# A chunkwise delta-rule recurrence on TensorE: the output products of one chunk are issued between the state products of the next

## The chip, the cores and the metric

The kernel runs on one core of one Trainium2 chip. The metric is device time in microseconds (us) of one execution, and the figure for a kernel is the median of its runs. Before the change that is 1708.27 us (three runs, 1707.21 to 1708.54).

## The reference, cut to what matters

The program is a two-layer encoder trunk for 512 frames of width 1024. The change lies in the gated DeltaNet heads of layer 0: 4 heads of 128 features, 8 chunks of 64 frames, one chunk after the other:

```python
def step(state, inp):
    u_c, wk_c, qk_c, qg_c, kt_c, dec_c = inp
    w = u_c - jnp.einsum('bhtd,bhde->bhte', wk_c, state)
    o = jnp.einsum('bhtd,bhde->bhte', qg_c, state) + jnp.einsum('bhtj,bhje->bhte', qk_c, w)
    state = dec_c[..., None, None] * state + jnp.einsum('bhtd,bhte->bhde', kt_c, w)
    return state, o
```

A chunk's w needs the state that the chunk before left. Its output o is needed by no later chunk, only by the normalisation and the output projection behind the loop.

## The kernel before, in words

Each engine has its own hand-written list of instructions, and semaphores join them; no scheduler moves anything. The recurrence is `rec_pe` (TensorE), `rec_dve` (VectorE) and `rec_act` (ScalarE), each a loop over the 8 chunks c. Two chunks share a 128-row tile i = c // 2: an even chunk's rows lie on partitions 0 to 63, an odd chunk's on 64 to 127 (`r`); `ro` is the other half.

For each chunk TensorE issues, in this order:

- L1325, "wk with state": per head a 128-row product to 64 output partitions, into banks 0 and 1 (two heads each). Between them L1328, "q with state", the first term of o, into bank 2 or 3 by the chunk's parity, on the other 64 output partitions. Both are done in two groups of two heads; a group waits for the state of its two heads (semaphore s_new), and L1325 of its second head counts r_ws up.
- L1333, "k with w": per head a product over the chunk's 64 rows to 128 output partitions, into banks 4 and 5. A group of two heads waits for its w (r_w) and counts r_kw up.
- L1336, "QK with w", the second term of o, added into the bank of L1328: per head a product over the same 64 rows to 64 output partitions. The last counts r_om up.

VectorE forms w from r_ws (L1350, two instructions of two heads), then the new state from r_kw (L1354, four instructions of one head); after chunks 3, 5 and 7 it also sums squares of an earlier output tile (L1376). w lies in two slots by parity, so L1350 of chunk c waits until r_om tells that chunk c - 2 is through. ScalarE copies o out of its bank (L1363, counts r_o) and squares it (L1366) after an odd chunk. L1325 of chunk c waits for the copy of chunk c - 2.

Behind the loop TensorE goes on with the output projection: 48 matmuls of the S5 half (L329 to L331) into banks 0 to 3, after r_o has counted all 8 chunks and GpSimd has split the S5 half (L1416, L1417, semaphore cat_s5); then the transposes of the normalised DeltaNet outputs (L1424), the DeltaNet half, and the rest of the program.

A fp32 matmul of these lines is recorded as two passes, each a weight load and a matmul: 4 heads give 8 records. The form that the profile prints before the operand shapes, such as 64*128, is rows by columns of the array that the instruction uses; 64*64 and 64*128 are L1336 and L1333, 128*64 is L1325 and L1328.

Of the kernel before, what the change touches and what calls it, by code (L numbers as in the profile page):

```python
# [10 lines left out]
ACT = mybir.ActivationFunctionType  # L11
AX = mybir.AxisListType.X

P = 128
# [19 lines left out]
GH = 4  # L34
GD = 128
NCH = SEQ // CHUNK
# [39 lines left out]
def build_program(nc, A):  # L76
    ctx = ExitStack()
    with ctx:
# [14 lines left out]
        ps = ctx.enter_context(nc.psum_tensor("ps", [P, 8, 512], F32))  # L93
# [32 lines left out]
        def named(name):  # L126

            if name in GOES_ON:
                return GOES_ON[name]
            head, _, tail = name.partition("_")  # L130
            for what, tags in SERIES.items():
                if head in tags and in_series(what, tail, head) is not None:
                    return f"{what}_{tail}", sum(in_series(what, tail, t) or 0 for t in tags[:tags.index(head)])
            if head[-1].isdigit() and f"{head[:-1]}_{tail}" in PER_LAYER:
                base_name = f"{head[:-1]}_{tail}"
                goes_on, n = GOES_ON.get(base_name, (base_name, 0))
                return goes_on, n + int(head[-1]) * PER_LAYER[base_name]
            return name, 0

        def sem(name):  # L140
            name = named(name)[0]
            if name not in sems:
                sems[name] = ctx.enter_context(nc.semaphore(name))
            return sems[name]


        def reg(at, *shape):
            n = 1
            for s in shape:
                n *= s  # L150
            v = sb[:, at - SB0:at - SB0 + n]
            if len(shape) == 2:
                v = v.rearrange("p (a b) -> p a b", a=shape[0])
            if len(shape) == 3:
                v = v.rearrange("p (a b c) -> p a b c", a=shape[0], b=shape[1])
            if len(shape) == 4:
                v = v.rearrange("p (a b c d) -> p a b c d", a=shape[0], b=shape[1], c=shape[2])
            return v
# [39 lines left out]
        CHUNKS = (slice(0, CHUNK), slice(CHUNK, P))  # L198
# [201 lines left out]
        def norm_pe(pe, t, x, h):  # L400

            n = x.shape[1]
            for k in range(KT):
                for i in range(n):
                    if k == 0:
                        pe.wait_ge(sem(f"{t}_hv"), after(f"{t}_hv", i + 1))
                    ins = pe.transpose(norm_bank(n, k)[:, i * P:(i + 1) * P], h[:, i, k * P:(k + 1) * P], ident)
                ins.then_inc(sem(f"{t}_turned"), 1)
# [224 lines left out]
        def logits_pe(pe):  # L633
            pe.wait_ge(sem("wab_lo"), 1)
            for k in range(KT):
                for part in range(2):
                    ins = pe.matmul(ps[0:4 * GH, 7, :], w_ab_split[:, k, :, :].rearrange("p a b -> p (a b)"), hT0[part][:, k, :],
                                    start=(k == 0 and part == 0), stop=(k == KT - 1 and part == 1))
            ins.then_inc(sem("logit_mm"), 1)
# [336 lines left out]
        q_gT = gd(TT, GH, P)  # L976
        AQ_T = gd(TT, 2, GH, CHUNK)
        U_m, Y_m, T_m, A_l = gd(TT, GH, CHUNK), gd(TT, GH, CHUNK), gd(TT, GH, CHUNK), gd(TT, GH, CHUNK)
        A_T, QK_T = AQ_T[:, :, 0], AQ_T[:, :, 1]
# [3 lines left out]
        state = gd(GH, GD)  # L983
        w_c = gd(2, GH * GD)
# [20 lines left out]
        u_n, wk_T, o_t = reg(qkv0, TT, GH, GD), reg(qkv0 + 2048, TT, GH, P), reg(qkv0 + 4096, TT, GH, GD)  # L1005
        flat3 = lambda a: a.rearrange("p a b -> p (a b)")
# [304 lines left out]
                              ps[:, 4 * (i % 2) + 2:4 * (i % 2) + 4, 0:SOLVE_W].rearrange("p c (h t) -> p c h t", h=GH)).then_inc(sem("wk_c"), 1)  # L1311


        def rec_pe(pe):
            for c in range(NCH):
                i, r, ro = c // 2, CHUNKS[c % 2], CHUNKS[1 - c % 2]
                for g in range(2):
                    pe.wait_ge(sem("s_new"), 1 + GH * (c - 1) + 2 * g + 2 if c else 1)
                    if c == 0 and g == 0:
                        pe.wait_ge(sem("u_c"), 2 * TT)  # L1320
                        pe.wait_ge(sem("wk_c"), TT)
                    if c >= 2 and g == 0:
                        pe.wait_ge(sem("r_o"), c - 1)
                    for h in (2 * g, 2 * g + 1):
                        ins = pe.matmul(ps[r, g, h * P:(h + 1) * P], wk_T[:, i, h, r], state[:, h, :], start=True, stop=True)  # L1325
                        if h == 2 * g + 1:
                            ins.then_inc(sem("r_ws"), 1)
                        pe.matmul(ps[ro, 2 + c % 2, h * P:(h + 1) * P], q_gT[:, i, h, r], state[:, h, :], start=(h == 0), stop=False,  # L1328
                                  skip_group_check=True)
                for g in range(2):  # L1330
                    pe.wait_ge(sem("r_w"), 2 * c + g + 1)
                    for h in (2 * g, 2 * g + 1):
                        ins = pe.matmul(ps[:, 4 + g, h * P:(h + 1) * P], k_t[r, i, h, :], w_c[r, c % 2, h * P:(h + 1) * P], start=True, stop=True)  # L1333
                    ins.then_inc(sem("r_kw"), 1)
                for h in range(GH):
                    ins = pe.matmul(ps[ro, 2 + c % 2, h * P:(h + 1) * P], QK_T[r, i, h, :], w_c[r, c % 2, h * P:(h + 1) * P],  # L1336
                                    start=False, stop=True, skip_group_check=True)
                ins.then_inc(sem("r_om"), 1)

        def rec_dve(v):  # L1340
            for c in range(NCH):
# [17 lines left out]
        def rec_act(a):  # L1359
            for c in range(NCH):  # L1360
                i, r = c // 2, CHUNKS[1 - c % 2]
                a.wait_ge(sem("r_om"), c + 1)
                a.activation(flat3(o_t[r, i]), ps[r, 2 + c % 2, :], ACT.Copy).then_inc(sem("r_o"), 1)  # L1363
                if c % 2 == 1:
                    a.wait_ge(sem("r_o"), c + 1)
                    a.activation(o_sq[:, i], o_t[:, i], ACT.Square).then_inc(sem("go_sq"), 1)  # L1366
# [1013 lines left out]
        @block.tensor  # L2380
        def _(pe):
            pe.wait_ge(sem("con_in"), 16)
            norm_pe(pe, "n0", x0, h0)
            ab_groups_pe(pe, 0, 3)
            logits_pe(pe)
            ab_groups_pe(pe, 4, 4)
            logits_turn_pe(pe)
            ab_groups_pe(pe, 5, 9)
            gates_pe(pe)
            ab_groups_pe(pe, 10, 12)  # L2390
            s5_tables_pe(pe)
            ab_groups_pe(pe, 13, 13)
            s5_tm_pe(pe)
            ab_groups_pe(pe, 14, 14)
            s5_states_pe(pe)
            ab_groups_pe(pe, 15, 19)
            gdn_squares_pe(pe)
            s5_out_pe(pe)
            s5_back_pe(pe)
            gdn_turn_pe(pe, 0)  # L2400
            gdn_prod_pe(pe, 0)
            s5_glu_pe(pe)
            pe.wait_ge(sem("glu_s"), 4)
            for i in range(TT):
                gdn_row_pe(pe, i)
                gdn_back_pe(pe, i)
                if i + 1 < TT:
                    gdn_turn_pe(pe, i + 1)
                    gdn_prod_pe(pe, i + 1)
            solve_pe(pe)  # L2410
            uw_pe(pe)
            rec_pe(pe)


            def cat_ready(k):
                if k == 0:
                    pe.wait_ge(sem("r_o"), NCH)
                    pe.wait_ge(sem("cat_s5"), 1)
                if k >= 4:
                    pe.wait_ge(sem("cat_lo"), after("cat_lo", k - 3))  # L2420

            rows_pe(pe, "mo", "abo0", cat, TT, 0, ready=cat_ready, between=lambda: gout_pe(pe))
            def mem_turn():
                pe.wait_ge(sem("mo_x"), after("mo_x", 4))
                norm_pe(pe, "m", mem_x, mem_x)

            rows_pe(pe, "mo", "abo1", cat, TT, 4, between=mem_turn)
            for l in range(DEPTH):
                if l == 0:
                    kv_pe(pe)  # L2430

                xq_pe(pe, l)
                xa_pe(pe, l)

                split_outproj_pe(pe, f"xo{l}", xo[l], oT[l], ready=lambda k: pe.wait_ge(sem(f"xa{l}_ov"), after(f"xa{l}_ov", k + 1)), between=lambda: turn_rows_pe(pe, f"f{l}", 0, f"xo{l}_x"))
                ffn_up_pe(pe, l)
                ffn_down_pe(pe, l)
                if l == 0:
                    ca_proj_pe(pe)
                    ca_turn_pe(pe)  # L2440
                    ca_pe(pe)
                    pe.wait_ge(sem("c_ol"), CH // 2)
                    split_outproj_pe(pe, "co", cao, c_oT, between=lambda: turn_rows_pe(pe, "x1", 0, "co_x"))
# [280 lines left out]
```

## Time and profile before

| what | value |
|---|---|
| median of three runs | 1708.27 us |
| profiled execution, its own time | 1708.71 us |
| its span | 1706.9 us |
| TensorE busy | 1648.6 us, 97% of the span |
| stretch of the recurrence | 284.4 to 311.1 us of the span, 8 chunks |
| TensorE matmul records in that stretch | 256 |
| granted TensorE clock in that stretch | 1.00 of full speed |

The span runs from the first to the last instruction that the profile holds; 1.8 us of the execution lie around it. Times in the rows below are microseconds from the start of the span. A matmul record's end is modelled, so spacing is read from the starts of records; busy shares of TensorE tell little, since a record lasts about 0.27 us even where the next starts 0.11 us after it.

### The profile page before, as it was taken

How to read it: one execution, taken by the hardware profiler on the slowest of the kernel's cores; microseconds unless marked ns; L12 is line 12 of the kernel's file. 1: busy time of each engine (PE TensorE's matmuls, PEld its weight loads, DVE VectorE, ACT ScalarE, POOL GpSimd, SP SyncE). 2: the span in 40 equal slices, each digit the busy share in tenths (PEclk: the TensorE clock that was granted, in tenths of full speed). 3: DMA queues.
4: the chain of work that ended last, by engine and by line, in shares of the span. 5: the costliest groups of instructions: out<-in, count | busy, mean ns of one | idle time of the engine just before them, and what ended most of it. 6: DMA issues, size and time to landing. Idle time of an engine off the chain costs nothing.

```text
span 1706.9 us, 22635 instructions
## 1 busy us (share of the span) xinstructions
PE 1648.6 (97%) x9358; PEld 1343.3 (79%) x9358; DVE 768.2 (45%) x1006; ACT 623.9 (37%) x1010; POOL 253.4 (15%) x315
## 2 busy tenths in 40 slices
PE   5989989999999999999999999999999999999999
PEld 4778788788878788888888887567887788888887
DVE  4658435555444444443225435773453444444222
ACT  6533433344434322221114336564452522222110
POOL 3863034010000211110000003110000011111000
PEclk9999899999999999999999999999999999999999
DMA  6610212034212333332223332322212243333221
GB/s 203 135 50 1 75 52 71 31 123 149 74 49 75 99 98 98 96 97 88 92 95 99 99 123 99 96 78 99 80 45 74 60 113 98 93 93 94 91 98 74
DMA packets 146801, 151.85 MB, mean 89 GB/s; under 512 B 8864, under 2 KB 109344, under 8 KB 146592
## 3 DMA queue, kind: packets, MB, share of 16 engines
q1 hardware_dynamic: 146720, 150.69, 28.9%
q8 instruction: 60, 0.98, 0.2%
q14 instruction: 21, 0.17, 0.0%
HBM read 147.53 MB, written 3.15 MB: 88 GB/s over the span
## 4 chain that ended last, share of the span: by engine, by line
PE 88%; DVE 6%; ACT 4%; issue 2%; POOL 0%; DMA 0%; SPq 0%; DVEq 0%; ACTq 0%; POOLq 0%
PE ps L329 24%; PE ps L331 24%; PE ps L330 24%; PE ps L2070 1%; PE ps L1730 1%; PE ps L425 1%; PE ps L2100 1%; DVE sb L610 1%; PE ps L1707 1%; PE ps L964 1%; DVE w_lo_ab L301 1%; PE ps L2088 1%; ACT sb L1741 1%; ACT sb L2159 1%; PE ps L1242 1%
## 5 line engine op out<-in xcount | busy, mean ns | idle before, releaser
L329 PE MATMUL ps<-h_hi,w_hi 128*128 128x512 f32 x864 | 338.7, 392 | 4.4 <-DVE w_lo L1904 3.9
L330 PE MATMUL ps<-h_lo,w_hi 128*128 128x512 f32 x864 | 337.2, 390 | 0.0
L301 DVE TENSOR_TENSOR w_lo<-raw,w_hi 128x2048 fp32r<-128x2048 f32 x66 | 155.0, 2349 | 341.7 <-ACT w_hi L297 341.7
L297 ACT ACTIVATE w_hi<-raw 128x2048 fp32r<-128x2048 f32 x84 | 160.8, 1915 | 377.1 <-PE ps L331 376.4
L331 PE MATMUL ps<-h_hi,w_lo 128*128 128x512 f32 x704 | 274.4, 390 | 0.0
L329 PEld LDWEIGHTS ps<-h_hi,w_hi 128*128 128x128 f32 x864 | 162.9, 189 | 39.2 <-issue 4.7
L330 PEld LDWEIGHTS ps<-h_lo,w_hi 128*128 128x128 f32 x864 | 162.9, 189 | 33.5
L1904 DVE TENSOR_TENSOR w_lo<-raw,w_hi 128x2048 fp32r<-128x2048 f32 x44 | 138.1, 3139 | 53.5 <-ACT w_hi L1886 53.5
L331 PEld LDWEIGHTS ps<-h_hi,w_lo 128*128 128x128 f32 x704 | 132.5, 188 | 27.8
L1886 ACT ACTIVATE w_hi<-raw 128x2048 fp32r<-128x2048 f32 x44 | 84.3, 1916 | 161.2 <-PE ps L331 161.2
L1914 POOL CAST a_hi<-up 128x512 f32 x44 | 27.0, 613 | 777.2 <-DVE up L1902 777.2
L329 PE MATMUL ps<-w_hi,a_hi 128*128 128x512 f32 x352 | 137.3, 390 | 1.7 <-DVE up L1902 1.7
L330 PE MATMUL ps<-w_lo,a_hi 128*128 128x512 f32 x352 | 137.0, 389 | 0.0
L331 PE MATMUL ps<-w_hi,a_lo 128*128 128x512 f32 x352 | 137.0, 389 | 0.0
L329 PE MATMUL ps<-w_hi,h_hi 128*128 128x512 f32 x320 | 125.0, 391 | 0.0
L331 PE MATMUL ps<-w_hi,h_lo 128*128 128x512 f32 x320 | 124.5, 389 | 0.0
L330 PE MATMUL ps<-w_lo,h_hi 128*128 128x512 f32 x320 | 124.5, 389 | 0.0
L1902 DVE TENSOR_TENSOR up<-up,ps 128x512 f32<-128x512 f32 x44 | 30.3, 688 | 192.6 <-PE ps L331 188.9
L1882 ACT ACTIVATE up<-up 128x512 f32<-128x512 f32 x44 | 27.8, 632 | 153.2 <-DVE up L1898 153.2
L329 PEld LDWEIGHTS ps<-w_hi,a_hi 128*128 128x128 f32 x352 | 66.1, 188 | 16.1 <-DVE up L1902 2.5
L331 PEld LDWEIGHTS ps<-w_hi,a_lo 128*128 128x128 f32 x352 | 66.1, 188 | 13.9
L330 PEld LDWEIGHTS ps<-w_lo,a_hi 128*128 128x128 f32 x352 | 66.1, 188 | 13.6
(378 smaller groups left out, 2697.3 us busy)
## 6 DMA issues: line engine op xcount, KB each, us to landing
raw<-in_f_w_gate SPq DMA_DIRECT2D x44, 512.0 KB, 4.0
raw<-in_f_w_up SPq DMA_DIRECT2D x44, 512.0 KB, 5.2
raw<-in_f_w_down SPq DMA_DIRECT2D x44, 512.0 KB, 4.2
raw<-in_xa_w_kv SPq DMA_DIRECT2D x16, 1024.0 KB, 5.0
raw<-in_c_w_qkv SPq DMA_DIRECT2D x12, 1024.0 KB, 5.1
raw<-in_ab_w_in SPq DMA_DIRECT2D x10, 1024.0 KB, 6.0
raw<-in_xa_w_q SPq DMA_DIRECT2D x8, 1024.0 KB, 5.0
raw<-in_xa_w_out SPq DMA_DIRECT2D x8, 1024.0 KB, 5.0
```

The lines of the kernel that those rows point to most:

```text
L297: a.activation(w_hi[:, n % 2, :], raw[n % 2], ACT.Copy).then_inc(sem("w_hi"), 1)
L301: v.tensor_tensor(w_lo(n)[:, n % 2, :], raw[n % 2], w_hi[:, n % 2, :].bitcast(F32), ALU.subtract).then_inc(sem("w_lo"), 1)
L329: pe.matmul(out, a[0], b[0], start=start, stop=False)
L330: pe.matmul(out, a[0], b[1], start=False, stop=False)
L331: return pe.matmul(out, a[1], b[0], start=False, stop=stop)
L425: ins = pe.transpose(ps[:, k, i * P:(i + 1) * P], x[:, i, k * P:(k + 1) * P], ident)
L610: ins = v.scalar_tensor_tensor(y[:, s:SEQ], b[:, 0:SEQ - s], pcol("conv", (3 - s) * 12 + n), y[:, s:SEQ], ALU.mult, ALU.add)
L1882: a.activation(gsil[:, s, :], gsil[:, s, :], ACT.Silu).then_inc(sem(f"f{l}_silu"), 1)
L1886: a.activation(w_hi[:, slot, :], raw[slot], ACT.Copy).then_inc(sem("w_hi"), 1)
L1902: v.tensor_tensor(prod[:, s, :], gsil[:, s, :], ps[:, 2 * s + 1, :], ALU.mult).then_inc(sem(f"f{l}_free"), 1)
L1904: v.tensor_tensor(w_lo(n0)[:, slot, :], raw[slot], w_hi[:, slot, :].bitcast(F32), ALU.subtract).then_inc(sem("w_lo"), 1)
L1914: g.tensor_copy(aT[0][:, at], prod[:, s, :]).then_inc(sem(f"f{l}_ahi"), 1)
```

## The change

The products of QK with w of chunk c - 1 are issued between the four products of k with w of chunk c, one behind each head, and no longer behind their own chunk. Since chunks alternate between the row halves, the two products of such a pair read different halves of the partitions. The outputs o go round four banks (2, 3, 6, 7) in place of two, so L1325 of chunk c waits for the copy of chunk c - 4, and the projection behind the loop waits for 6 copies in place of 8. Chunk 0 has no chunk before it; the products of chunk 7 follow the loop. r_kw is counted up by the second k product of a group, so before the QK product that is now behind it. The number of instructions is the same.

```diff
+        O_BANKS = (2, 3, 6, 7)
+
         def rec_pe(pe):
+
+            def om(c, h):
+                r, ro = CHUNKS[c % 2], CHUNKS[1 - c % 2]
+                return pe.matmul(ps[ro, O_BANKS[c % 4], h * P:(h + 1) * P], QK_T[r, c // 2, h, :], w_c[r, c % 2, h * P:(h + 1) * P],
+                                 start=False, stop=True, skip_group_check=True)
+
             for c in range(NCH):
...
-                    if c >= 2 and g == 0:
-                        pe.wait_ge(sem("r_o"), c - 1)
+                    if c >= 4 and g == 0:
+                        pe.wait_ge(sem("r_o"), c - 3)
...
                 for g in range(2):
                     pe.wait_ge(sem("r_w"), 2 * c + g + 1)
                     for h in (2 * g, 2 * g + 1):
                         ins = pe.matmul(ps[:, 4 + g, h * P:(h + 1) * P], k_t[r, i, h, :], w_c[r, c % 2, h * P:(h + 1) * P], start=True, stop=True)
-                    ins.then_inc(sem("r_kw"), 1)
-                for h in range(GH):
-                    ins = pe.matmul(ps[ro, 2 + c % 2, h * P:(h + 1) * P], QK_T[r, i, h, :], w_c[r, c % 2, h * P:(h + 1) * P],
-                                    start=False, stop=True, skip_group_check=True)
-                ins.then_inc(sem("r_om"), 1)
+                        if h == 2 * g + 1:
+                            ins.then_inc(sem("r_kw"), 1)
+                        if c > 0:
+                            ins = om(c - 1, h)
+                            if h == GH - 1:
+                                ins.then_inc(sem("r_om"), 1)
+            for h in range(GH):
+                ins = om(NCH - 1, h)
+            ins.then_inc(sem("r_om"), 1)
...
             def cat_ready(k):
                 if k == 0:
-                    pe.wait_ge(sem("r_o"), NCH)
+                    pe.wait_ge(sem("r_o"), NCH - 2)
```

TensorE's list inside the loop, before: the k products of a chunk (L1333), its QK products (L1336), and the first product of the next chunk with the state (L1325).

```order
L1333 MATMUL ps<-sb 128x128 [waits r_w]
L1333 MATMUL ps<-sb 128x128
L1333 MATMUL ps<-sb 128x128 [waits r_w]
L1333 MATMUL ps<-sb 128x128
L1336 MATMUL ps<-sb 64x128 x4
L1325 MATMUL ps<-sb 64x128 [waits r_o,s_new]
```

The same place in the changed kernel, chunks 1 to 7; the k products are now on L1341, the QK products of the chunk before on L1320, and the first product with the state on L1333.

```order
L1341 MATMUL ps<-sb 128x128 [waits r_w]
L1320 MATMUL ps<-sb 64x128
L1341 MATMUL ps<-sb 128x128
L1320 MATMUL ps<-sb 64x128
L1341 MATMUL ps<-sb 128x128 [waits r_w]
L1320 MATMUL ps<-sb 64x128
L1341 MATMUL ps<-sb 128x128
L1320 MATMUL ps<-sb 64x128
L1333 MATMUL ps<-sb 64x128 [waits s_new]
```

Four instructions of one line followed by four of another have become eight that alternate; the first product with the state still comes behind all eight.

TensorE's list at the end of the loop, before: the last group of k products of chunk 7, its QK products and the projection (L329).

```order
L1333 MATMUL ps<-sb 128x128 [waits r_w]
L1333 MATMUL ps<-sb 128x128
L1336 MATMUL ps<-sb 64x128 x4
L329 MATMUL ps<-w_hi,s_hi 128x512 [waits cat_s5,r_o,w_lo]
L330 MATMUL ps<-w_lo_abo,s_hi 128x512
```

The same place in the changed kernel.

```order
L1341 MATMUL ps<-sb 128x128 [waits r_w]
L1320 MATMUL ps<-sb 64x128
L1341 MATMUL ps<-sb 128x128
L1320 MATMUL ps<-sb 64x128 x5
L329 MATMUL ps<-w_hi,s_hi 128x512 [waits cat_s5,r_o,w_lo]
L330 MATMUL ps<-w_lo_abo,s_hi 128x512
```

Five QK products stand in one row there: the last of chunk 6 and the four of chunk 7. The wait of L329 keeps its three semaphores, with a smaller count for r_o.

## Rows read from the trace of the kernel before

**Rows 1.** The page's first part, and the stretch of the recurrence in the windows view.
```profile
PE 1648.6 (97%) x9358; PEld 1343.3 (79%) x9358; DVE 768.2 (45%) x1006; ACT 623.9 (37%) x1010; POOL 253.4 (15%) x315
...
core 0: us, PE busy (x) PEld busy (x) DVE busy (x) ACT busy (x) POOL busy (x), PEclk, DMA share, GB/s
284.40:311.10 26.70, 25.62 (x256) 21.30 (x256) 16.88 (x51) 9.16 (x13) 15.38 (x4) 1.00 0.37 119
```

**Rows 2.** The chain that ended last, in order of time: chunk 1, and the end.
```profile
288.89 1.16 PE ps L1333 x8
290.05 1.01 PE ps L1336 x8
291.06 0.25 PE ps L1325
...
291.75 0.42 DVE sb L1350
292.18 0.04 issue
292.22 1.16 PE ps L1333 x8
...
308.87 1.16 PE ps L1333 x8
310.03 1.01 PE ps L1336 x8
311.04 0.73 issue
311.77 0.47 PE ps L329
```

**Rows 3.** Timeline of chunk 0 into chunk 1: start, duration, engine, line, form, records.
```profile
285.63 1.16 PE L1333 MATMUL ps<-sb 64*128 64x128 f32 x8
286.37 1.12 DVE L1354 SCALAR_TENSOR_TENSOR sb<-sb,ps 128x128 f32<-128x128 f32 x4 [0.43 <-PE ps L1333]
286.71 1.08 PE L1336 MATMUL ps<-sb 64*64 64x128 f32 x8
287.73 0.32 PE L1325 MATMUL ps<-sb 128*64 128x128 f32 x1
...
288.21 0.27 PE L1325 MATMUL ps<-sb 128*64 128x128 f32 x1
...
288.41 0.86 DVE L1350 TENSOR_TENSOR sb<-sb,ps 64x256 f32<-64x256 f32 x2 [0.92 <-PE ps L1325]
```

**Rows 4.** Timeline in narrow windows, where the form changes: single passes of chunk 1.
```profile
288.89 0.48 PE L1333 MATMUL ps<-sb 64*128 64x128 f32 x2
...
289.78 0.27 PE L1333 MATMUL ps<-sb 64*128 64x128 f32 x1
...
289.98 0.43 PE L1336 MATMUL ps<-sb 64*64 64x128 f32 x2
...
290.80 0.27 PE L1336 MATMUL ps<-sb 64*64 64x128 f32 x1
...
290.99 0.32 PE L1325 MATMUL ps<-sb 128*64 128x128 f32 x1
...
291.00 0.32 PE L1328 MATMUL ps<-sb 128*64 128x128 f32 x1
```

**Rows 5.** Timeline ahead of the recurrence: L1292 and L1296 alternate between the row halves.
```profile
282.23 0.28 PE L1292 MATMUL ps<-sb 64*64 64x128 f32 x2
...
282.44 0.33 PE L1296 MATMUL ps<-sb 64*128 64x64 f32 x2
...
282.44 1.11 PE L1296 MATMUL ps<-sb 64*128 64x64 f32 x16
```

**Rows 6.** Instructions of L1354 and L1376, and the timeline after chunk 7's state.
```profile
L1354 DVE SCALAR_TENSOR_TENSOR sb<-sb,ps x32: 340/343/349, 286.4 to 310.4; 128x128 f32<-128x128 f32 x32
...
309.62 1.15 DVE L1354 SCALAR_TENSOR_TENSOR sb<-sb,ps 128x128 f32<-128x128 f32 x4 [0.43 <-PE ps L1333]
...
310.68 0.68 DVE L1376 TENSOR_REDUCE sb<-sb 128x4 f32<-128x512 f32 x1
311.08 0.59 ACT L1363 ACTIVATE sb<-ps 64x512 f32<-64x512 f32 x1 [2.74 <-PE ps L1336]
```

**Rows 7.** Timeline: GpSimd's last step for the projection, the normalisation, the transposes.
```profile
296.78 4.52 POOL L1417 TENSOR_TENSOR s_lo<-sb,s_hi 128x2048 fp32r<-128x2048 f32 x1
...
314.50 2.50 DVE L1385 TENSOR_TENSOR sb<-sb 128x512 f32<-128x512 f32 x4
...
322.77 1.91 PE L1424 MATMUL ps<-sb 128*128 128x128 f32 x16
```

**Rows 8.** What TensorE waited for from 311 us on: total, times, longest.
```profile
PE ps L329 <- DVE w_lo L1904: 3.9, 2, 2.5
PE ps L2088 <- ACT sb L2116: 3.6, 3, 1.9
PE ps L329 <- DVE w_lo L301: 2.2, 3, 0.9
```

More of the change, by code:

```diff
@@ L1327, in rec_pe @@
                             ins.then_inc(sem("r_ws"), 1)
-                        pe.matmul(ps[ro, 2 + c % 2, h * P:(h + 1) * P], q_gT[:, i, h, r], state[:, h, :], start=(h == 0), stop=False,
+                        pe.matmul(ps[ro, O_BANKS[c % 4], h * P:(h + 1) * P], q_gT[:, i, h, r], state[:, h, :], start=(h == 0), stop=False,
                                   skip_group_check=True)
@@ L1362, in rec_act @@
                 a.wait_ge(sem("r_om"), c + 1)
-                a.activation(flat3(o_t[r, i]), ps[r, 2 + c % 2, :], ACT.Copy).then_inc(sem("r_o"), 1)
+                a.activation(flat3(o_t[r, i]), ps[r, O_BANKS[c % 4], :], ACT.Copy).then_inc(sem("r_o"), 1)
                 if c % 2 == 1:
```

## Prediction

> **What bounds the kernel now.** I read the page's first part first: TensorE is busy 97% of the span, and nothing else over half [rows 1]. The windows view then gives the recurrence 26.70 us, 1.6% of the span, at a granted clock of 1.00, the upper level of 2.4 GHz [rows 1]. So whatever the change is worth lies in 26.7 us, and the question is what sets the pace there. The chain that ended last answers it [rows 2]. Reckoned from one chunk's first k product (288.89) to the next one's (292.22) a chunk takes 3.33 us, in four pieces: k products, QK products, products with the state, w on VectorE. The QK products stand in this chain only because they are ahead of the next chunk's L1325 in TensorE's list; nothing in the loop reads what they make. Take them out and the state update is next. In chunk 0 L1354 starts 0.74 us behind the first k product [rows 3]; each lasts 0.34 [rows 6] and four take 1.12 [rows 3], so one follows the other at 0.26 and the second ends at 0.74 + 0.26 + 0.34 = 1.34. L1325 of the next chunk, which needs those two heads, could start about 0.05 later (as L1333 at 288.89 follows the first of two L1350, 0.43 us each, from 288.41 [rows 3, 4]), at 1.39 us. It starts at 287.73, 2.10 us behind [rows 3]. So at most 0.70 us a chunk is to be had, if the QK products cost nothing where they now stand.
>
> **What an alternation costs.** That is the term on which everything rests. Two kinds of step have rows.
>
> Within one form, passes on different row halves run side by side. L1296 alternates between the halves, on the same 128 columns and into different banks: two of its records fill 0.33 us though one lasts 0.32, and 16 fill 1.11 us [rows 5], while L1333, always on one half in a chunk, needs 1.16 us for 8 [rows 3].
>
> Where the form changes, all rows show a stop. The last L1333 starts at 289.78, the first L1336 at 289.98: 0.20 us, where L1333's own step is (1.16 - 0.48) / 6 = 0.11 [rows 3, 4]. Neither waits for anything. L1336 to L1325 is 0.20 too (290.80 to 290.99) [rows 4], and L1292 to L1296, from 64*64 to 64*128, the direction that is new here, 0.20 to 0.21 (282.23 to 282.44) [rows 5]. Behind a stop the first pass also shows its weight load: L1333's first two passes fill 0.48, so the second comes 0.48 - 0.27 = 0.21 after the first, and L1336's comes 0.43 - 0.27 = 0.16 after [rows 4].
>
> In the changed list L1341 (64*128) and L1320 (64*64) alternate head by head. What the rows cannot tell is whether the stop holds back the other row half too: in each of these changes the new form also follows the old one on the same half. I take it that it does, because the nearest row (L1292 to L1296, with both halves in work) shows no record of the new form ahead of the stop on either half.
>
> The page "TensorEngine Tiling (Array Packing)" of the Trainium skill, section Key Properties, speaks against this change: it says that switching the tiling mode, and not just the tile, drains the engine, and its list of modes has 64×128 and 64×64 as two. By that rule each of the alternations would stop the engine; it gives no price, and the trace agrees at the changes of form above, 0.20 us each, but shows none with the halves kept apart.
>
> **The sum.** One head's pair then takes 0.21 (two passes of k) + 0.20 (change) + 0.16 (two passes of QK) + 0.20 (change) = 0.77 us, four take 3.08, and L1333, the next chunk's first product, starts 3.08 us behind the first k product in place of 2.10.
>
> - Chunks 1 to 6: +0.98 each, 5.9 us. The state doesn't add to it: the last k product's second pass starts at 3 x 0.77 + 0.21 = 2.52, VectorE follows 0.31 later (0.74 less the 0.21 + 2 x 0.11 to the pass that released it), the last two L1354 end at 2.83 + 0.26 + 0.34 = 3.43, and the product that needs them is due at 3.08 + 0.48 (287.73 to 288.21 [rows 3]) = 3.56.
> - Chunk 0 has no QK products between and goes at the state's pace: -0.70 us.
> - L1376 stands behind the state update of chunks 3 and 5 in VectorE's list and ends 0.59 after it (311.36 against 310.77) [rows 6], at 4.02. L1350 would be due at 3.08 + about 0.76 (290.99 to 291.75) [rows 2, 4] = 3.84. So about 0.2 us of it shows, twice: +0.4. Before it showed none.
> - The end: now 2.90 us from chunk 7's first k product (308.87) to L329 (311.77), 0.73 of them the wait for the copy of o [rows 2]. After: chunk 6's last QK pass at 2.88, eight passes of chunk 7 in the same form at 0.11, from about 2.83 to 3.60, one change of form 0.20: 3.80. The copy's wait is gone, since 6 copies are done by then. +0.9.
>
> 5.9 - 0.7 + 0.4 + 0.9 = 6.5 us. The copies (0.59 us each [rows 6]), the bank waits and the slot of w cost nothing: four banks give a copy two more chunks, and L1320 of a chunk is through before the L1333 that precedes the next w.
>
> Does it reach the end? The S5 half that L329 needs is ready at 301.30, 10 us ahead, and would be 5 ahead even if L329 came 5 us early; the normalisation ends at 317.0 while the transposes start at 322.77 behind 48 matmuls [rows 7]. Behind that TensorE's longest wait is 2.5 us, on work released by TensorE itself [rows 8]. So I carry the sum to the end in full.
>
> The profiled execution took 1708.71 us, the median is 0.44 lower. The profiled time becomes 1715.2, the median 1714.8; I give 1715.0, and 1712 to 1718 for this case by itself: a change of form at 0.15 or 0.25 us moves 6 x 8 x 0.05 = 2.4 us, and the spread of the runs adds some tenths.
>
> **Rivals.**
>
> *The halves are independent, faster.* If a stop concerns only the half on which the form changes, then in a chunk each half keeps one form, QK goes beside k as in L1296 [rows 5], and the 0.70 us a chunk are won: 7 x 0.70 = 4.9. Given back: L1376 now ends at 1.34 + 0.52 + 0.59 = 2.45 against L1350 due at 1.39 + 0.70, about 0.37 twice, 0.7. The end: chunk 7's QK products follow the last pair, 1.07 to 1.90, then 0.20: 2.10 in place of 2.90, -0.8. Sum -5.0 us, 1703.3. For it speaks that the rows show no stop confined to one half or not; against it that both halves of L1296 start together, 0.20 behind both halves of L1292 [rows 5]. It decides at one point: whether the first L1320 starts within 0.02 us of an L1341, or 0.20 behind it. Chance 0.20.
>
> The page "TensorE: Matmul & The Clock Gate" of the Trainium skill, Part 3, The mechanism, stands on this rival's side: matmuls on different row groups start about 4 ns apart, and weight loads overlap matmuls in flight where the row group differs. The trace agrees within one form, and no row shows it across two.
>
> *The stop stays, but the weights are loaded under it.* The other half's weights could be in place when the stop ends; then a head's pair is 0.11 + 0.20 + 0.11 + 0.20 = 0.62, four 2.48, +0.38 x 6 = 2.3, -0.7, L1376 0.6, the end 3.25 against 2.90: together +2.5 us, 1710.8, within 0.2%. Against it: the first two passes behind every stop are 0.16 or 0.21 apart [rows 4]. Chance 0.08.
>
> *The two passes of a product are not kept together*, so the form changes with every pass. A pass then pays its own load: 0.31 for k, 0.25 for QK, 1.12 a head, 4.5 a chunk: 6 x 2.4 + 0.6 + 1.0, about +16 us, 1724. L1325 and L1328 do interleave pass by pass, 0.01 apart [rows 4], but within one form. Chance 0.04.
>
> **Numbers.** The stop on every alternation 0.68, independent halves 0.20, loads under the stop 0.08, change with every pass 0.04. A difference of 0.2%, 3.4 us, is about what a measurement of this kernel can tell from no change. The first and last are slower by more than that, 0.72; loads under the stop is within it, 0.08; independent halves faster, 0.20. Leaving out the last case and the lower half of the independent one, the range is 1703 to 1719; as cases of both signs are in it, the likeliest one's own range is 1712 to 1718.
>
> **What would show it.** In the profile of the changed kernel: L1320 about 0.20 us behind L1341 and L1341 0.20 behind L1320, with form changes 7 times in a chunk; the first k products of chunks 1 to 7 4.2 to 4.5 us apart, but chunks 0 and 1 only 2.6; L1376 ending after L1333's release; no issue gap ahead of L329; L329 first near 318 us. I am wrong if pairs of L1341 and L1320 start together, with chunks at 2.6 to 3.0 us and L329 near 306.8, or if the recurrence is longer and the end is not.

## The result, and the profile after

The changed kernel takes 1727.7 us in the median (four runs, 1724.33 to 1729.2) against 1707.74 us before (four runs, 1706.85 to 1708.54): a ratio of 1.0116, 95% interval 1.01 to 1.0132. It is slower, as forecast, but by 20 us where 6.5 were worked out, and the time lies above the range.

The stops are where they were expected. In narrow windows of the timeline of the changed kernel, chunk 1 (rows as in [rows 4]; L1341 is a k product, L1320 a QK product):

```profile
287.39 0.48 PE L1341 MATMUL ps<-sb 64*128 64x128 f32 x2
287.81 0.43 PE L1320 MATMUL ps<-sb 64*64 64x128 f32 x2
288.17 0.48 PE L1341 MATMUL ps<-sb 64*128 64x128 f32 x2
...
288.69 0.61 DVE L1366 SCALAR_TENSOR_TENSOR sb<-sb,ps 128x128 f32<-128x128 f32 x2 [0.84 <-PE ps L1341]
290.24 0.60 DVE L1366 SCALAR_TENSOR_TENSOR sb<-sb,ps 128x128 f32<-128x128 f32 x2 [0.94 <-PE ps L1341]
```

A pair of k and QK products of one head takes 288.17 - 287.39 = 0.78 us (0.77 was reckoned). The first L1320 starts 0.42 behind the first L1341, so 0.42 - (0.48 - 0.27) = 0.21 behind its second pass, although it works on the other row half. VectorE's state update has come apart into two and two heads (before, four in a row [rows 3]).

What was not expected shows in the page's clock line and in the windows view of the changed kernel (stretch, length, busy us and instructions of TensorE, its weight loads, VectorE, ScalarE, GpSimd, then the granted clock, DMA share, GB/s):

```profile
PEclk9999999699999999999999999999999999999999
```

```profile
287.39:291.71 4.32, 4.19 (x33) 2.78 (x32) 2.10 (x7) 0.59 (x1) 4.32 (x2) 1.00 0.19 32
295.00:335.96 40.96, 40.96 (x177) 27.42 (x175) 13.42 (x37) 8.37 (x14) 5.37 (x2) 0.50 0.07 26
318.29:325.53 7.24, 7.24 (x34) 4.69 (x33) 2.05 (x6) 1.22 (x2) 0.00 (x0) 0.50 0.01 2
336.00:400.00 64.00, 61.17 (x282) 49.79 (x282) 35.21 (x46) 26.52 (x54) 4.66 (x2) 1.00 0.24 83
```

Chunk 1 takes 4.32 us at the full clock (3.33 before [rows 2]). Then from 295.00 to 335.96 us the clock is granted at 0.50, 1.2 GHz, where before the whole recurrence had 1.00 [rows 1]; a chunk there, the third row, takes 7.24 us. The timeline of that chunk shows the same passes stretched:

```profile
318.29 0.79 PE L1341 MATMUL ps<-sb 64*128 64x128 f32 x2
319.01 0.68 PE L1320 MATMUL ps<-sb 64*64 64x128 f32 x2
319.63 0.79 PE L1341 MATMUL ps<-sb 64*128 64x128 f32 x2
...
332.15 0.79 PE L329 MATMUL ps<-w_hi,s_hi 128*128 128x512 f32 x1
```

A head's pair takes 1.34 us in place of 0.78. L329 starts at 332.15, where before it started at 311.77 [rows 2]; that is the 20 us. The windows view from the first product with the state to L329, of the changed kernel and of the kernel before, and a third row from the kernel before, far behind the recurrence:

```profile
283.62:332.15 48.53, 48.04 (x256) 31.93 (x256) 18.00 (x51) 9.09 (x12) 15.35 (x4) 0.62 0.19 66
284.43:311.77 27.34, 25.62 (x257) 21.31 (x257) 17.14 (x51) 9.77 (x14) 15.38 (x4) 1.00 0.36 117
1362.00:1367.00 5.00, 4.20 (x12) 3.34 (x13) 3.19 (x4) 3.68 (x3) 1.89 (x2) 0.66 0.65 181
```

The clock is back at 336, after some 4 us of the projection's 512-column matmuls. From the transposes behind the projection to the end (344.93 to 1727.4 us, before 322.77 to 1706.9) the changed kernel takes 1.7 us less: the kernel before has one more short fall of the clock there, the third row. Such short falls, elsewhere than in the recurrence, are in every profile, not always at the same places, so a difference of 1 or 2 us between two kernels can come from them.

So there are theories to tell apart. **Mine**: the alternation costs about 6.5 us by its stops; the stops also leave TensorE with so little done in the stretch that the clock is halved, and that costs the rest. **The rivals**: something else in the change (the shift by a chunk, the four banks, the waits) costs the time; or the stops cost all of it and the clock only accompanies it.

### The profile page after: what moved, and what is told of

It is laid out like the page before. It is cut to its first block, busy times and chain, and to the rows that moved or that the text cites. A ratio compares the mean times of both kernels' runs of the same rounds, so it can differ in the third digit from the quotient of the medians.

```text
span 1727.4 us, 22633 instructions
## 1 busy us (share of the span) xinstructions
PE 1670.3 (97%) x9358; PEld 1353.9 (78%) x9358; DVE 769.0 (45%) x1006; ACT 623.6 (36%) x1010; POOL 253.2 (15%) x315
## 4 chain that ended last, share of the span: by engine, by line
PE 88%; DVE 6%; ACT 4%; issue 2%; POOL 0%; DMA 0%; SPq 0%; ACTq 0%; DVEq 0%; POOLq 0%
PE ps L329 24%; PE ps L331 24%; PE ps L330 24%; PE ps L2082 1%; PE ps L1341 1%; PE ps L1742 1%; PE ps L425 1%; PE ps L1320 1%; PE ps L2112 1%; DVE sb L610 1%; PE ps L1719 1%; PE ps L964 1%; DVE w_lo_ab L301 1%; PE ps L2100 1%; ACT sb L1753 1%
## 5 line engine op out<-in xcount | busy, mean ns | idle before, releaser
L329 PE MATMUL ps<-h_hi,w_hi 128*128 128x512 f32 x864 | 337.9, 391 | 4.3 <-DVE w_lo L1916 3.9
L329 PEld LDWEIGHTS ps<-h_hi,w_hi 128*128 128x128 f32 x864 | 162.6, 188 | 39.1 <-issue 5.3
L329 PE MATMUL ps<-w_hi,a_hi 128*128 128x512 f32 x352 | 137.3, 390 | 1.7 <-DVE up L1914 1.7
L329 PE MATMUL ps<-w_hi,h_hi 128*128 128x512 f32 x320 | 125.0, 391 | 0.0
L329 PEld LDWEIGHTS ps<-w_hi,a_hi 128*128 128x128 f32 x352 | 66.1, 188 | 16.2 <-DVE up L1914 2.5
```

Of the source, the lines that this page charges most:

```text
L329: pe.matmul(out, a[0], b[0], start=start, stop=False)
```

## The experiments

Ten runs follow, of seven new kernels (one of them twice) and of the change itself (twice). They came in three sets, each with the kernel before on the same chip. Before took 1706.77 us (22 runs) beside the first four (QK behind k, two heads, k in halves, filler), 1706.68 us (14 runs) beside the next four (QK widened, the cut by itself, doubled filler, the change again), and 1707.27 us (10 runs, one of them an outlier of 4270.02) beside the last two (filler and change side by side).

### The alternation taken out

```diff
                     for h in (2 * g, 2 * g + 1):
                         ins = pe.matmul(ps[:, 4 + g, h * P:(h + 1) * P], k_t[r, i, h, :], ...)
-                        if h == 2 * g + 1:
-                            ins.then_inc(sem("r_kw"), 1)
-                        if c > 0:
-                            ins = om(c - 1, h)
...
+                    ins.then_inc(sem("r_kw"), 1)
+                if c > 0:
+                    for h in range(GH):
+                        ins = om(c - 1, h)
+                    ins.then_inc(sem("r_om"), 1)
```

> The changed kernel with the four QK products of the chunk before placed behind the four k products, so that one change of form is left between them in place of seven; banks, waits and the shift by one chunk stay as in the change. Theory (the alternation itself does the harm, by the stops and then by the clock): chunks back at 3.3 us, 0.7 us won in chunk 0, the granted clock at 1.00 through the recurrence, about 1707 us. Rival (the shift by one chunk, the four banks or the new waits do it): chunks over 4 us, a clock of 0.5, about 1727 us.

Measured: 1704.89 us (10 runs), ratio to before 0.9988, interval 0.9979 to 0.9998. The windows view of the recurrence:

```profile
284.00:310.40 26.40, 25.22 (x256) 20.97 (x256) 17.14 (x51) 8.89 (x12) 15.37 (x4) 1.00 0.35 121
```

The clock holds. The shift, the four banks and the new waits cost nothing; the median is even 1.9 us lower. In the traces 0.9 us of that lie between the first product with the state and L329 (26.42 us against 27.34), with chunk 0 shorter and L329 no longer waiting for the last copies. The whole loss is in the order of eight instructions.

### Fewer changes of form

```diff
-                        if c > 0:
-                            ins = om(c - 1, h)
...
+                    if c > 0:
+                        for h in (2 * g, 2 * g + 1):
+                            ins = om(c - 1, h)
```

> The changed kernel with the alternation by two heads: two k products, two QK products, two and two; three changes of form in a chunk in place of seven. Theory (each change of form costs a stop and the exposed weight loads, and the clock falls only where the stops take much of TensorE's time): a chunk of 3.6 us at the full clock, 0.33 more than before, and about 1710 us if the clock holds; if it falls in the last chunks, 1714 to 1724 us. Rival (the loss is one price for any interleaving, whatever the number of changes): about 1727 us.

Measured: 1707.32 us (10 runs), ratio 1.0004, interval 0.9994 to 1.0013. The timeline of one chunk, and the windows view of the recurrence:

```profile
290.89 0.71 PE L1341 MATMUL ps<-sb 64*128 64x128 f32 x4
291.53 0.65 PE L1320 MATMUL ps<-sb 64*64 64x128 f32 x4
292.10 0.71 PE L1341 MATMUL ps<-sb 64*128 64x128 f32 x4
292.74 0.65 PE L1320 MATMUL ps<-sb 64*64 64x128 f32 x4
293.32 0.32 PE L1333 MATMUL ps<-sb 128*64 128x128 f32 x1
```

```profile
284.00:312.00 28.00, 26.82 (x251) 20.59 (x246) 17.37 (x51) 8.22 (x12) 15.36 (x4) 1.00 0.34 113
```

From the first k product to the next chunk's L1333 it is 2.43 us, against 2.10 before [rows 3] and 3.10 with seven changes (4 x 0.775): four changes less save 0.67 us, 0.17 each. In the trace the first product with the state to L329 takes 28.63 us, 1.3 more than before. The time is 2.7 us under the expectation's 1710, and within the noise that of before. The clock stayed at 1.00 in the recurrence. So the price goes by the number of changes, and with three of them the clock holds.

### One form for both, first way: the k products in halves

```diff
-                        ins = pe.matmul(ps[:, 4 + g, h * P:(h + 1) * P], k_t[r, i, h, :], w_c[...], start=True, stop=True)
+                        for cs in CHUNKS:
+                            ins = pe.matmul(ps[cs, 4 + g, h * P:(h + 1) * P], k_t[r, i, h, cs], w_c[...], start=True, stop=True)
```

> The changed kernel with each k product cut into two products of 64 output partitions, so that k and QK products have one form, 64*64, and alternate without a change of form. Theory (only the change of form stops the engine; within a form the row halves run side by side): QK products start about 0.01 us beside k products, chunks of 2.6 to 3.0 us set by the state update on VectorE, the clock at 1.00, about 1703 us. Rival (products of different halves with different operands do not run side by side here): 24 passes a chunk one after the other at 0.11, 2.6 us in place of 2.1, about 1711 us or more.

Measured: 1699.49 us (4 runs, 1699.26 to 1700.78), ratio 0.9958, interval 0.9941 to 0.9974, 7.3 us faster than before and 3.5 under the expectation's 1703. It beats both kernels. The timeline of a chunk's k and QK products, L1342 the halves of the k products and L1320 the QK products, and the windows view:

```profile
290.52 0.33 PE L1342 MATMUL ps<-sb 64*64 64x128 f32 x2
290.53 0.32 PE L1320 MATMUL ps<-sb 64*64 64x128 f32 x1
290.68 0.28 PE L1342 MATMUL ps<-sb 64*64 64x128 f32 x2
290.69 0.27 PE L1320 MATMUL ps<-sb 64*64 64x128 f32 x1
290.79 0.28 PE L1342 MATMUL ps<-sb 64*64 64x128 f32 x2
290.80 0.27 PE L1320 MATMUL ps<-sb 64*64 64x128 f32 x1
```

```profile
284.20:305.80 21.60, 18.99 (x320) 14.29 (x320) 16.54 (x51) 9.10 (x12) 15.40 (x4) 1.00 0.44 147
```

Three passes start within 0.01 us, two halves of a k product and a QK product; the next three follow 0.16 us later, and from there on three more every 0.11 us. QK costs nothing here. The recurrence takes 21.60 us from the first product with the state to L329, 5.7 less than the 27.34 before. The rest of the 7.3 lies outside: in this profile the clock does not fall behind the recurrence, and in that of before it does, at 1093 and at 1363 us. The chain of waits of this kernel, from chunk to chunk, now runs through VectorE's state update:

```profile
291.22 0.03 DVE sb L1367
...
291.48 0.35 DVE sb L1367
291.83 0.04 issue
291.88 0.32 PE ps L1333
```

### One form for both, second way: the QK products widened

```diff
-                return pe.matmul(ps[ro, O_BANKS[c % 4], h * P:(h + 1) * P], QK_T[r, c // 2, h, :], ...)
+                at = (2 * (c // 2) + 1) * GH * CHUNK + h * CHUNK - ro.start
+                return pe.matmul(ps[:, O_BANKS[c % 4], h * P:(h + 1) * P], AQ_flat[r, at:at + P], ...)
```

> The changed kernel with each QK product inside the loop widened to 128 columns, 64 of them a neighbour's weights whose results land on the half of the output bank that nobody reads; so both lines have the form 64*128 and none is cut. Theory (what stops the engine is the change of form, whichever side is fitted to the other): QK products about 0.01 us beside k products, chunks of 2.6 to 2.8 us, the clock at 1.00, about 1700 us as with the k products in halves. Rival (64*64 products are what runs side by side, 64*128 ones contend for the columns that they share): 16 passes one after the other at 0.11, chunks near 3.0 us or more, 1703 to 1708 us.

Measured: 1700.12 us (5 runs), ratio 0.9958, interval 0.9944 to 0.9972. The timeline of four passes, L1346 a k product, L1325 a QK product:

```profile
290.64 0.37 PE L1346 MATMUL ps<-sb 64*128 64x128 f32 x1
290.65 0.37 PE L1325 MATMUL ps<-sb 64*128 64x128 f32 x1
290.86 0.27 PE L1346 MATMUL ps<-sb 64*128 64x128 f32 x1
290.86 0.27 PE L1325 MATMUL ps<-sb 64*128 64x128 f32 x1
```

The list of instructions is that of the change, in the same order and number; inside the loop only the width of one operand, and with it of the result, differs, half of it useless. From the first product with the state to L329 it takes 22.12 us, 5.2 less than before. It is 32 us faster than the change on the same chip (1732.09). So neither the overlap of the row halves nor the order is at fault by itself: the form is. That the two share all 128 columns does no harm, as L1296 had shown [rows 5].

### The cut by itself

```diff
-                        ins = pe.matmul(ps[:, 4 + g, h * P:(h + 1) * P], k_t[r, i, h, :], ...)
+                        for cs in CHUNKS:
+                            ins = pe.matmul(ps[cs, 4 + g, h * P:(h + 1) * P], k_t[r, i, h, cs], ...)
```

The same edit as above, in the kernel before.

> The kernel before with nothing but the k products cut into halves of 64 output partitions; QK products stay behind their own chunk's k products. Theory (the gain of the kernel with k in halves comes from the overlap, and the form alone is worth one stop a chunk): a chunk of about 3.2 us in place of 3.33, 1 to 1.5 us faster than before. Rival (the cut itself is what gains, for instance because both halves of a product end sooner): 5 to 7 us faster than before.

Measured: 1705.04 us (10 runs), ratio 0.999, interval 0.998 to 1.0. A chunk takes 3.11 us (288.80 to 291.91). Of the 7.3 us of the kernel with k in halves, the cut alone gives 1.6 and the shift with its banks alone 1.9 (first run); if they add, some 4 us are left for the overlap. By the traces, from the first product with the state to L329, it is 5.7 in all, 1.7 for the cut (25.68 us) and 0.9 for the shift, which leaves 3.1. The expectation was 3.2 us and a gain of 1 to 1.5. In its timeline (L1334 k, L1337 QK products) the QK products start 0.93 us behind the first k product, 1.09 before (288.89 to 289.98 [rows 2, 4]):

```profile
288.80 1.09 PE L1334 MATMUL ps<-sb 64*64 64x128 f32 x16
289.73 1.03 PE L1337 MATMUL ps<-sb 64*64 64x128 f32 x8
291.91 1.09 PE L1334 MATMUL ps<-sb 64*64 64x128 f32 x16
```

### More work, less time: the clock by itself

```diff
+                for _ in range(1):
+                    pe.matmul(ps[r, O_BANKS[c % 4], 0:2 * P], con[:, 0:CHUNK], con[:, 0:2 * P], start=True, stop=True, skip_group_check=True)
                 for g in range(2):
                     pe.wait_ge(sem("r_w"), 2 * c + g + 1)
```

> The changed kernel, all its stops kept, with one useless product more in each chunk (128 rows, 64 output partitions, 256 columns, fp32: two passes, about 0.43 us) while TensorE waits for w; it writes into the unused half of the partitions of an output bank. Theory (of the loss about 6.5 us are stops and the rest is the fallen clock, which falls because TensorE does little in the stretch): if the product is enough to hold the clock, about 1716 us with a clock of 1.00 in the recurrence, faster than the changed kernel though it does more; if not, 1729 us or more. Rival (the clock has no part in it, the stops just cost three times what was reckoned): the time of the changed kernel plus 8 times about 0.25 us, about 1729 us, whatever the clock does.

Measured: 1715.12 us (7 runs: five between 1712.58 and 1715.85 at mean clocks of 0.991 to 0.994, and two of 1726.3 and 1727.94 at 0.985 and 0.984). The profiled one took 1712.58; its windows view of the recurrence and of the stretch right behind, and its timeline (L1339 is the filler, L1343 a k product):

```profile
280.30:315.60 35.30, 35.05 (x272) 23.59 (x272) 17.10 (x51) 8.96 (x12) 15.36 (x4) 1.00 0.27 90
315.69:320.00 4.31, 4.31 (x13) 3.43 (x13) 2.01 (x5) 3.06 (x6) 0.00 (x0) 0.60 0.00 0
```

```profile
288.68 0.59 PE L1339 MATMUL ps<-sb 128*64 128x256 f32 x2
289.21 0.48 PE L1343 MATMUL ps<-sb 64*128 64x128 f32 x2
...
289.98 0.48 PE L1343 MATMUL ps<-sb 64*128 64x128 f32 x2
```

All stops of the change are there, at the same spacing (289.98 - 289.21 = 0.77). In this profile the clock stays at 1.00 through the recurrence, though the kernel does more than the changed one, and falls for a short time just behind it (second row). In the two longest runs, of which there is no trace, the mean clock is the changed kernel's. The changed kernel had not run beside these, so both follow once more on one chip:

> The changed kernel with the useless product of 256 columns a chunk once more, now with the changed kernel itself on the same chip. Theory: about 1713 to 1716 us where the clock holds in the recurrence, with some runs near 1727 where it does not; the median at least 9 us below that of the changed kernel beside it. Rival (the gap between the filler and the change was one between two chips): no gap, or the filler slower by its own 2 us.

> The changed kernel on the chip of the run with the filler. Theory: 1724 to 1732 us, a mean clock of 0.979 to 0.985 in every run. Rival (as in the run beside it): a median within 3 us of the kernel with the filler.

Measured: with the filler 1716.71 us (7 runs), the change 1729.87 us (4 runs, 1727.19 to 1733.68, mean clocks 0.979 to 0.983): the useless product takes 13 us off the median. Run by run the time with the filler goes with the mean clock: 1714.91 at 0.993, 1715.65 and 1716.12 and 1716.71 at 0.992, 1721.09 at 0.987, 1729.83 at 0.983, 1732.03 at 0.982. The profiled run is the one of 1721.09; in its windows view the clock fell for a part of the recurrence only (the second row reaches into the projection):

```profile
282.00:300.00 18.00, 17.15 (x111) 11.82 (x112) 7.01 (x21) 5.48 (x5) 15.35 (x4) 0.73 0.53 176
300.00:340.00 40.00, 38.86 (x227) 27.60 (x226) 17.36 (x45) 8.50 (x14) 0.00 (x0) 0.91 0.00 1
```

The change beside it, in the same stretches but for the start:

```profile
284.00:300.00 16.00, 15.07 (x124) 10.35 (x126) 7.92 (x25) 5.24 (x6) 14.22 (x4) 1.00 0.57 198
300.00:340.00 40.00, 40.00 (x172) 27.81 (x171) 13.52 (x34) 7.16 (x12) 1.13 (x1) 0.57 0.00 1
```

One program, one list of stops, and 17 us between its fastest and its slowest run, in the order of the mean clock: that is the clock's price. The filler does not hold the clock surely; it makes the fall rarer and shorter.

A larger filler:

```diff
-                    pe.matmul(ps[r, O_BANKS[c % 4], 0:2 * P], con[:, 0:CHUNK], con[:, 0:2 * P], ...)
+                    pe.matmul(ps[r, O_BANKS[c % 4], 0:4 * P], con[:, 0:CHUNK], con[:, 0:4 * P], ...)
```

> The changed kernel, all stops kept, with the useless product of 512 columns a chunk in place of 256 (two passes of 0.21 us more columns each). Theory (more work in the stretch holds the clock): the clock at 1.00 in the recurrence in every run, about 1714 + 8 times 0.43 = 1718 us with a small spread, so more work than the smaller filler and yet no run near 1727. Rival (what the filler did to the clock was chance): some runs near 1727 or above, at a mean clock of 0.985.

Measured: 1722.19 us (4 runs: 1718.63, 1720.2, 1724.18, 1724.24, at mean clocks of 0.990 to 0.992), 10 us below the change on the same chip (next section). None has the mean clock of the changed kernel. But the expectation failed in part: the median is 4 us over its 1718, the spread is wider, and in the profiled run the clock held through the first seven chunks only. It fell in the last one, which begins at 316.07 and reaches L329 at 323.77:

```profile
281.00:316.00 35.00, 33.87 (x246) 20.85 (x246) 15.13 (x44) 9.12 (x11) 15.35 (x4) 1.00 0.26 91
316.00:323.77 7.77, 7.77 (x45) 4.85 (x43) 3.08 (x9) 1.81 (x3) 0.00 (x0) 0.72 0.00 1
```

So twice the filler does not hold the clock surely either, and its own time (a chunk of 4.97 us, against 4.55 with the small one) eats more of what it saves.

### The change once more

No edit: the changed kernel itself, on the chip of the doubled filler.

> The changed kernel itself, on the chip of the other runs. Theory: 1724 to 1729 us and a mean clock near 0.983 in every run, so that the kernel with a filler is faster on the same chip. Rival (the chip on which the change was timed was a slow one): 1714 us or less, with the clock at 1.00 through the recurrence.

Measured: 1732.09 us (4 runs, 1724.48 to 1732.19, mean clocks 0.979 to 0.985), ratio to before 1.0148. The profiled one, of 1724.48, lost the clock later; its windows view, and from its timeline the last product with the state and the first k product of chunks 3 and 4:

```profile
284.00:303.90 19.90, 18.90 (x152) 12.94 (x152) 9.88 (x30) 5.61 (x6) 15.36 (x4) 1.00 0.46 159
303.95:331.26 27.31, 27.31 (x116) 18.56 (x115) 9.32 (x25) 6.64 (x11) 0.00 (x0) 0.50 0.00 1
```

```profile
296.15 0.27 PE L1333 MATMUL ps<-sb 128*64 128x128 f32 x1
296.57 0.49 PE L1341 MATMUL ps<-sb 64*128 64x128 f32 x2
...
300.48 0.27 PE L1333 MATMUL ps<-sb 128*64 128x128 f32 x1
300.99 0.48 PE L1341 MATMUL ps<-sb 64*128 64x128 f32 x2 [0.23 <-DVE sb L1362]
```

The same program had its clock halved for 27.31 us here and for 40.96 us in the first profile. With five chunks at the full clock (but for the last 0.2 us of the fifth), this profile also gives the terms of the sum that the first could not. Both rivals fall: the shift and the banks by the first run, the clock as a mere companion by the filler, small and large.

## Why the prediction was wrong

Its direction and the mechanism of the stops held, and at the full clock their sum was right nearly term by term. The step that failed is that the stops were priced at a clock of 1.00 to the end of the recurrence: a change of the clock was put at nothing, without a reason. The traces showed a clock of 0.50 for 27 to 41 us instead, which in the first profile cost 14.8 us up to L329.

- **The pace before, and what is to be had in chunk 0**: right. From one L1333 or L1325 to the next chunk's, chunk 0 takes 2.60 us in the changed kernel and 3.29 before, 0.69 less (0.70 forecast).
- **A change of form stops the other row half too**: right. That was the choice on which the forecast rested, and no row of before showed it. L1320 starts 0.21 us behind the last pass of L1341 on the other half, and no longer does so once the forms are equal. The rival of independent halves falls as put, but its overlap is what one gets with one form, and its 5.0 us are close to the 5.2 and 5.7 that the traces then show up to L329 (6.6 and 7.3 in the medians).
- **0.98 us a chunk**: right. At the full clock the chunks take 4.27 to 4.33 us in place of 3.3.
- **L1376 shows by 0.2 us behind chunk 3**: it shows, by half of that. In the second profile chunk 4's first k product starts 0.51 us behind the last product with the state, chunk 3's 0.42, so 0.09 are L1376's. Chunk 4 takes 4.51 us and chunk 3 4.33; the other half of the difference falls behind chunk 4's last QK pass, where the clock was already at 0.50.
- **The end, +0.9**: right as far as it shows. In the profile with the small filler, from the last chunk's first product with the state to L329 is 5.21 us; less the 0.23 by which that filler lengthens a chunk (4.55 against 4.32) that is 4.98, against 4.13 before: 0.85.
- **"Does it reach the end?"**: here it failed. The working took the granted clock of 1.00 from the rows of before [rows 1] and carried it over, with the full-clock prices of its passes and stops, to a kernel in which TensorE does less in the same stretch. At 1.00 the sum of these measured terms is about 5.5 us for the seven chunks (chunks 5 and 6, which no profile of the change shows at the full clock, taken as 3 and 4) and 0.85 for the end, 6.4, where 6.5 was forecast. The runs with the small filler in which the clock held bear it out: 1714.87 and 1715.08 us at 0.993, less 8 x 0.23 for the filler, are 6.3 and 6.5 over the 1706.77 beside them. But from the first product with the state to L329 the changed kernel took 48.53 us in place of 27.34, 21.2 more (it began 0.8 earlier in the span). The other 14.8 are the clock at 0.50: four chunks of 7.1 to 7.24 us in place of 4.3 to 4.4, and a last stretch of 8.53 in place of 4.98. Behind that, from L329 to the transposes, it costs 1.8 more (12.78 us, before 11.00 [rows 2, 7]), and the one fall of the clock less behind them gives 1.7 back. No rival had a change of the clock in it, so the range did not either, and of the signs named, chunks of 4.2 to 4.5 us held only up to the fall, and L329 near 318 us did not come.
- **Rivals of the loads under the stop and of a change with every pass**: both fall by the timeline of chunk 1: the second pass of a product comes 0.21 (k) and 0.16 us (QK) after the first, and the two passes of a product stay together.

What stays open: what exactly makes the chip halve the clock (the little work in the stretch, or the many stops as such, which the filler also spreads over a longer chunk), and why at 295, 304 and 300 us in the three profiles of the change. Shown is only that the same stops with a useless product in each chunk lost it less often and for less long, that three changes of form kept it up, and that seven without the filler lost it, in all three profiles and by the mean clocks (0.979 to 0.985) in all twelve runs.

## What to carry to other kernels

Here, small products on different row halves of TensorE's array ran side by side as long as rows by columns of the form were the same, and stopped the whole engine when they differed, even on disjoint rows; so make the forms equal before interleaving, by cutting the wider product or by padding the narrower one. When a change thins out TensorE's work in a stretch, ask what becomes of the clock there: a loss of 6.4 us became one of 20. And try the coarser order too: with QK behind k, the same banks and waits gained about 1 us in the recurrence without any overlap.

## What the runs showed of the hardware that was not expected

- The clock fell to 0.50 while TensorE had, from the start of the recurrence on, no more than 0.53 us between the starts of two matmuls: it was never idle for long, just slowed by stops. In the three profiles of the change it came back only behind the recurrence, after 3.8 to 4.6 us of the projection's wide matmuls.
- Useless matmuls made a kernel faster: 1716.71 against 1729.87 us on the same chip, by the clock alone, and one program ran between 1714.91 and 1732.03 us with it.
- Three passes run at once where a k product's two column halves and a QK product's row half share one form, 0.11 us for the three; and a product widened with useless weights still starts together with its neighbour (290.86 us for both), in a kernel of 1700.12 us.
- The Trainium skill's page "TensorEngine Tiling (Array Packing)", section Key Properties, says that a change of mode, and not of tile, drains the engine. The trace agrees, with 0.20 us from the last pass to the first of the new form, and a first pass that also shows its weight load.
